# A three-block transformer kernel on one core: a second output tile begun later, earlier fills, roots by pairs, sums on GpSimd, and later weight copies before the last projection

## What is computed

```python
# first block
h = rms_norm(x, norm1_g); z = h @ w_in          # GLU input, q, k, v, gate logits
a = silu(rms_norm(conv31(val * sigmoid(gate)), conv_norm_g)); y_a = a @ w_conv_out
q, k = rms_norm per head; o = 3 dilated windows of attention, mixed by their sums
x = x + (g_a * y_a + g_b * (o @ w_attn_out)) @ w_out
x = x + (silu(u_gate) * u_val) @ w_down         # u = conv3(rms_norm(x) @ w_up)
# second block, layer 0 (sparse mixer): top-128 keys per query by 8 index heads
x = layer_norm(ALPHA * x + (o * silu(g)) @ w_out_a, ln_g0, ln_b0)
# layer 1 (stick-breaking mixer): weights from a cumulative log_sigmoid of the scores
x = layer_norm(ALPHA * x + (o * silu(g)) @ w_out_b, ln_g1, ln_b1)
```

## Time and profile before

| what | value |
|---|---|
| median of 3 runs | 1541.31 us (1541.19 to 1543.64) |
| the profiled execution | 1542.46 us |
| its span, first to last instruction | 1540.5 us |
| PE busy | 1515.3 us, 98% |
| DVE busy | 1152.0 us, 75% |
| ACT busy | 887.0 us, 58% |
| POOL busy | 768.8 us, 50% |
| granted TensorE clock | 0.998 |

### The profile page before, as it was taken

The page is one execution under the profiler, slowest core; times in us unless marked ns, Lnnn a source line. Parts: engine busy times, 40 slices in busy tenths (PEclk is TensorE's granted clock), DMA queues, the critical chain, the costliest instruction groups (busy, mean ns, idle before and its releaser), DMA issues.

```text
span 1540.5 us, 21821 instructions
## 1 busy us (share of the span) xinstructions
PE 1515.3 (98%) x7792; PEld 1293.6 (84%) x7792; DVE 1152.0 (75%) x2064; ACT 887.0 (58%) x1544; POOL 768.8 (50%) x726
## 2 busy tenths in 40 slices
PE   9999999999999999999999999999999999999997
PEld 7888899988888888888888888887888988888877
DVE  5999999998664687437717559967777828988977
ACT  6445788787433344324324464689995327777753
POOL 2232345435465477557747563456655424444443
PEclk9999999999999999999999999999999999999999
DMA  7889765665332222323222278856457945456551
GB/s 222 194 186 203 165 137 130 146 161 126 123 107 91 91 96 96 110 83 110 96 96 89 96 180 188 177 130 140 110 126 177 202 106 132 109 123 137 109 121 59
DMA packets 60299, 203.26 MB, mean 132 GB/s; under 512 B 6816, under 2 KB 9376, under 8 KB 60192
## 3 DMA queue, kind: packets, MB, share of 16 engines
q0 software_dynamic: 19008, 69.21, 26.3%
q1 hardware_dynamic: 40896, 132.14, 25.8%
q10 hardware_dynamic: 288, 0.52, 0.1%
HBM read 199.75 MB, written 2.10 MB: 131 GB/s over the span
## 4 chain that ended last, share of the span: by engine, by line
PE 84%; DVE 7%; ACT 5%; DMA 2%; issue 1%; POOL 1%; DVEq 0%; SPq 0%; POOLq 0%; ACTq 0%
PE bank L368 82%; PE bank L374 2%; DVE r L407 1%; DMA w_raw<-in_weights 1%; ACT k_both L378 1%; ACT prob L378 1%; ACT w_hi L378 1%; DVE pt_lo L395 1%; DMA w_lo<-in_weights 1%; DVE prob L1288 0%; ACT pt_hi L378 0%; DVE r L395 0%; DVE q_both L407 0%; DVE score L1875 0%; ACT soft L378 0%
## 5 line engine op out<-in xcount | busy, mean ns | idle before, releaser
L414 POOL TENSOR_TENSOR w_lo<-w_raw,w_hi 128x512 fp32r<-128x512 f32 (+1 forms) x190 | 278.5, 1485 | 210.3 <-ACT w_hi L378 210.3
L378 ACT ACTIVATE w_hi<-w_raw 128x1024 fp32r<-128x1024 f32 (+2 forms) x206 | 213.9, 1041 | 278.7 <-PE bank L368 253.3
L368 PE MATMUL bank<-x_hi,w_hi 128*128 128x512 f32 x872 | 346.6, 398 | 1.3 <-DVE k_lo_first L407 0.6
L368 PE MATMUL bank<-x_hi,w_lo 128*128 128x512 f32 x872 | 340.6, 391 | 0.6 <-DMA w_lo<-in_weights 0.4
L368 PE MATMUL bank<-x_lo,w_hi 128*128 128x512 f32 x872 | 340.1, 390 | 0.0
L368 PEld LDWEIGHTS bank<-x_hi,w_lo 128*128 128x128 f32 x872 | 163.7, 188 | 37.0 <-POOL w_lo L414 0.8
L368 PEld LDWEIGHTS bank<-x_hi,w_hi 128*128 128x128 f32 x872 | 163.9, 188 | 33.4 <-ACT k_both L378 1.0
L368 PEld LDWEIGHTS bank<-x_lo,w_hi 128*128 128x128 f32 x872 | 164.2, 188 | 29.8
L621 POOL DMA_DIRECT2D w_lo<-in_weights x132 | 117.0, 894 | 120.4 <-ACT w_lo L378 96.3
L368 PE MATMUL bank<-a_hi,w_hi 128*128 128x512 f32 x416 | 162.0, 389 | 0.0
L368 PE MATMUL bank<-a_hi,w_lo 128*128 128x512 f32 x416 | 161.8, 389 | 0.0
(11 more groups left out here) (230 smaller groups left out, 3403.5 us busy)
## 6 DMA issues: line engine op xcount, KB each, us to landing
w_raw<-in_weights SPq DMA_DIRECT2D x223, 512.0 KB, 3.4
w_lo<-in_weights POOLq DMA_DIRECT2D x132, 512.0 KB, 6.6
alibi<-in_alibi SPq DMA_DIRECT2D x16, 256.0 KB, 3.9
w_raw<-in_weights SPq DMA_DIRECT2D x8, 384.0 KB, 3.0
r<-in_x SPq DMA_DIRECT2D x8, 256.0 KB, 6.1
r<-in_x SPq DMA_DIRECT2D x4, 512.0 KB, 6.2
out_y<-r SPq DMA_DIRECT2D x16, 128.0 KB, 1.8
w_raw<-in_weights ACTq DMA_DIRECT2D x2, 256.0 KB, 4.2
```

Of the source, the lines that this page charges most:

```text
L368: return e.matmul(out, lhsT, rhs, start=start, stop=stop, skip_group_check=resumed)
L378: return self.act.run(lambda e: e.activation(out, in_, func, **kw), after, 0.07 + size(out) * 0.00086 + 0.09 * len(kw))
L414: return self.pool.run(lambda e: e.tensor_tensor(out, a, b, op), after, cost)
```

## The change

1. `two_tiles`: the first tile's units k run four ahead of the second's while the heads run, and the second tile takes its bank only at its first unit (`LEAD`).
2. `blank_scores`: the fills of `score` and `select` are put on DVE four planner microseconds after the feed-forward block, not at the start of `index_scores`.
3. `rsqrt`: y and g = m*y lie side by side, and one operation updates both; a root is 8 dependent operations (guess, g, then 2, 2 and 2) where it was 10.
4. `SHORT`: the planner counts at least 0.18 for a DVE operation of `v_tt`, `v_ts`, `v_stt` (before 0.07 for tiny ones). `LATER` is 0.5, not 1.5.
5. `sum_x`: in the last projection GpSimd adds x_hi and x_lo of tiles 4 to 7 (in the place of x_hi), so that `mix_evict` needs one DVE operation there, not two.
6. The ones used for column sums hold 1/D, so three multiplications by 1/D go; in `half_norm` a copy and a subtraction from the bank stand for two scalings and a subtraction.
7. `slot_ready`: `out_b` chunks in slots 5 and 6 also wait for the last pair's o parts.
8. `half_norm` of the last half: `keep_busy(3)` in front of the last tile's column sums. The first half's results start every 1.2, not 1.5.

```diff
-LATER = 1.5
+LATER = 0.5
+SHORT = 0.18
+LEAD = 4
@@ Block.__init__
+        self.x_sums = at("x_sums", 44, [KT, S])
@@ v_tt (v_ts and v_stt alike)
-        cost = 0.07 + size(out) * 0.00106
+        cost = max(SHORT, 0.07 + size(out) * 0.00106)
@@ slot_ready
         if self.slots[c] >= 3:
-            scores, weights = yield from self.know(self.phase_done, more_slots(self.plan[c])[0])
+            scores, weights, outputs = yield from self.know(self.phase_done, more_slots(self.plan[c])[0])
             after += yield from self.know(scores if self.slots[c] in AFTER_SCORES else weights, HEADS - 1)
+            if self.plan[c][0] == "out_b" and self.slots[c] in AFTER_WEIGHTS:
+                after += yield from self.know(outputs, PAIRS - 1)
@@ two_tiles
-        for key in keys:
-            begin(key)
-        for k in range(n_k - 1):
+        ahead = LEAD if self.in_heads else 0
+        order = sorted(((k, n) for k in range(n_k - 1) for n in range(len(keys))), key=lambda u: (u[0] if u[1] else u[0] - ahead, u[1]))
+        for k, n in order:
             while known is not None and k not in known and self.in_heads:
                 yield "idle"
-            for c, b in zip(cs, bs):
-                tok = self.unit(c, b, k, hi, lo, ready, False, used is not None and c == cs[-1])
...
+            while n == len(cs):
+                begin(keys[n])
+            second = used is not None and n == len(keys) - 1
+            tok = self.unit(cs[n], bs[n], k, hi, lo, ready, False, second)
...
@@ rsqrt(self, m, gy, t, ready)
+        g, y = gy[:, 0, :], gy[:, 1, :]
         tok = self.v_ts(y.bitcast(I32), m.bitcast(I32), -0.5, MAGIC, ALU.mult, ALU.add, [ready])
-        for _ in range(3):
-            tok = self.v_tt(t, y, y, ALU.mult, [tok])
-            tok = self.v_stt(t, t, -0.5, m, ALU.mult, ALU.mult, [tok])
-            tok = self.v_stt(y, t, 1.5, y, ALU.add, ALU.mult, [tok])
+        tok = self.v_tt(g, m, y, ALU.mult, [tok])
+        both = t.rearrange("p (o n) -> p o n", o=1).to_broadcast([P, 2, t.shape[-1]])
+        for n in range(3):
+            tok = self.v_stt(t, g, -0.5, y, ALU.mult, ALU.mult, [tok])
+            if n < 2:
+                tok = self.v_stt(gy, both, 1.5, gy, ALU.add, ALU.mult, [tok])
+            else:
+                tok = self.v_stt(y, t, 1.5, y, ALU.add, ALU.mult, [tok])
@@ rms
-        tok = self.v_ts(m, b.ap[:, 0:NT], 1.0 / D, eps, ALU.mult, ALU.add, [tok])
+        tok = self.v_ts(m, b.ap[:, 0:NT], eps, None, ALU.add, after=[tok])
@@ constants
-        self.ones_ready = self.v_fill(self.ones, 1.0)
+        self.ones_ready = self.v_fill(self.ones, 1.0 / D)
@@ index_scores, and a stream blank_scores started in sparse_mixer before the kiwi and qi tiles
+    def blank_scores(self):
+        yield self.hid_used
+        yield 4.0
         t0 = self.v_fill(self.score[:, :], 0.0, self.hid_used)
...
+    def index_scores(self):
+        t0 = self.got(self.blank, 0)
@@ sum_x, started by project_and_norm when last_norm is set, for tiles 4 to 7
+    def sum_x(self, used):
+        for c in self.x_summed:
+            hi, lo = self.x_hi[:, c, :].bitcast(F32), self.x_lo[:, c, :].bitcast(F32)
+            yield [used]
+            self.x_sum[c] = [self.p_tt(self.x_sums[:, c, :], hi, lo, ALU.add, [used])]
+            yield 1.4
@@ mix_evict
+        summed = (yield from self.know(self.x_sum, c)) if c in self.x_summed else []
+        x = self.x_sums[:, c, cols] if summed else self.x_hi[:, c, cols].bitcast(F32)
+        t = self.v_stt(u, x, 2.0 * ALPHA, b.ap[:, 0:n], ALU.mult, ALU.add, [t] + self.v_split[PAIRS - 1] + summed)
         b.release([t])
-        t = self.v_stt(u, self.x_lo[:, c, cols].bitcast(F32), 2.0 * ALPHA, u, ALU.mult, ALU.add, [t])
+        if not summed:
+            t = self.v_stt(u, self.x_lo[:, c, cols].bitcast(F32), 2.0 * ALPHA, u, ALU.mult, ALU.add, [t])
@@ half_norm
+        if half and self.last_norm:
+            yield from self.keep_busy(3)
         yield [t_u]
...
-        t1 = self.v_ts(mu, b.ap[:, 2 * half:2 * half + 2], 1.0 / D, None, ALU.mult, after=[t])
-        t2 = self.v_ts(m, b.ap[:, NT + 2 * half:NT + 2 * half + 2], 1.0 / D, None, ALU.mult, after=[t])
-        b.release([t2])
-        t = self.v_tt(w, mu, mu, ALU.mult, [t1])
-        t = self.v_tt(m, m, w, ALU.subtract, [t2, t])
+        t1 = self.v_copy(mu, b.ap[:, 2 * half:2 * half + 2], [t])
+        w_done = self.v_tt(w, mu, mu, ALU.mult, [t1])
+        t = self.v_tt(m, b.ap[:, NT + 2 * half:NT + 2 * half + 2], w, ALU.subtract, [t, w_done])
+        b.release([t])
@@ build
-        self.project_and_norm("out_b", 4, "ln_g1", "ln_b1", self.result, (1.5, 0.4))
+        self.project_and_norm("out_b", 4, "ln_g1", "ln_b1", self.result, (1.2, 0.4))
```

More of the change, by code:

```diff
@@ L397, in v_ts @@
     def v_ts(self, out, a, s1, s2, op0, op1=None, after=()):
-        cost = 0.07 + size(out) * 0.0008
+        cost = max(SHORT, 0.07 + size(out) * 0.0008)
         if op1 is None:
@@ L403, in v_stt @@
     def v_stt(self, out, a, s, b, op0, op1, after=()):
-        cost = 0.07 + size(out) * 0.00115
+        cost = max(SHORT, 0.07 + size(out) * 0.00115)
         if not (banked(a) or banked(b)):
@@ L676, in begin @@
             bs[-1].open = True
-        for key in keys:
-            begin(key)
-        for k in range(n_k - 1):
+        ahead = LEAD if self.in_heads else 0
+        order = sorted(((k, n) for k in range(n_k - 1) for n in range(len(keys))), key=lambda u: (u[0] if u[1] else u[0] - ahead, u[1]))
+        for k, n in order:
             while known is not None and k not in known and self.in_heads:
                 yield "idle"
-            for c, b in zip(cs, bs):
-                tok = self.unit(c, b, k, hi, lo, ready, False, used is not None and c == cs[-1])
-                if used is not None and c == cs[-1]:
-                    used[k] = [tok]
-                self.tick()
-                yield
+            while n == len(cs):
+                begin(keys[n])
+            second = used is not None and n == len(keys) - 1
+            tok = self.unit(cs[n], bs[n], k, hi, lo, ready, False, second)
+            if second:
+                used[k] = [tok]
+            self.tick()
+            yield
         for n, key in enumerate(late):
@@ L858, in spread, with rms @@
         return tok
-    def rms(self, acc, ready, eps, y):
+    def rms(self, acc, ready, eps, gy):
         yield ready
@@ L1053, in norm @@
             tok = yield from self.know(sums, KT - 1)
-            b, t, t_inv = yield from self.rms(acc[:, :], [tok, self.ones_ready, self.ident_in], 1e-6, self.h_inv)
+            b, t, t_inv = yield from self.rms(acc[:, :], [tok, self.ones_ready, self.ident_in], 1e-6, self.h_gy)
             self.wide_inv = self.ext[1]
@@ L1611, in conv_norm @@
                 yield from self.pad_known(c)
-            bank, bt, _ = yield from self.rms(self.ext[2][:, :], [self.conv_sq], 1e-6, self.stat_y)
+            bank, bt, _ = yield from self.rms(self.ext[2][:, :], [self.conv_sq], 1e-6, self.stat_gy)
             yield [bt]
@@ L1683, in norm @@
             tok = yield from self.know(self.sq_tok, KT - 1)
-            b, t, _ = yield from self.rms(self.ext[2][:, :], [tok], 1e-6, self.stat_y)
+            b, t, _ = yield from self.rms(self.ext[2][:, :], [tok], 1e-6, self.stat_gy)
             yield [t]
@@ L1824, in index_scores @@
             t0 = self.v_fill(self.score[0:64, a + 64:a + P], -BIG, [t0])
-        tok = {i: t0 for i in range(1, NT)}
         t1 = self.v_fill(self.select[:, 0:P], 0.0)
         self.select_ready[0] = [self.v_fill(self.select[0:64, 64:P], BIG, [t1])]
+        self.blank[0] = t0
+    def index_scores(self):
+        t0 = self.got(self.blank, 0)
+        tok = {i: t0 for i in range(1, NT)}
         rel_free = {}
@@ L1916, in ready @@
             return self.got(x_ready, k)
+        self.blank = {}
+        self.start(self.blank_scores())
         keys = [("kiwi", 0)] + [("qi", c) for c in range(4)]
@@ L1999, in project_and_norm @@
             self.start(self.half_norm(half, self.u_ready, self.u_sum, self.u_sq, *norm))
+        if self.last_norm:
+            self.x_summed = range(FIRST_HALVED[name], KT)
+            self.start(self.sum_x(self.chunk_done[self.plan.index(("gb", PAIRS - 1))]))
         hi, lo = (lambda k: self.o_hi[:, k, :]), (lambda k: self.o_lo[:, k, :])
```

26 lines of the change are left out of this document (15 added, 11 removed).

## The result

The changed kernel takes 1548.66 us (median of 6 runs, 1546.96 to 1552.74), the kernel before beside it 1542.26 (6 runs, 1541.19 to 1543.64): a ratio of 1.0038, 95% interval 1.0028 to 1.0048. It is slower by 6 us where 3.4 us were to be won.

What follows compares the result with a forecast made beforehand. PE, busy 98% of the span, was taken as the bound, with at most 25 us idle to win. Terms -2.2 + 0.4 - 0.1 - 1.2 + 0.2 - 0.5 = -3.4 gave a median of 1537.9 us, range 1534.7 to 1541.8.

Steps and rivals of the forecast that it cites:

- the rescheduling: LEAD in the two other mixers and SHORT everywhere move waits without a direction: 0, bounds -1.5 and +1.5 us.
- the cover of GpSimd's sums: Last projection: four additions of 1.29 us, 5.2 us on POOL, hidden under tiles 4 and 5 (5.7 us and more).
- the tail: Behind the last tile, from 1527: GpSimd's sums, constants, keep_busy(3) and pace give -0.1 us, bounds -0.9 and +0.9.
- Roots, LATER, SHORT: First heads move forward and fill waits: -1.2 us, bounds 0 and -2.0; separately +0.2 in the three RMS norms.
- the fills: Score fills move from the start of the index scores to idle DVE time: -0.5 us, bounds 0 and -1.6.
- The wait before k_both,q_both: First heads, near 178: this wait of PE was to be under 0.5 us if the prediction was right.
- The seam: Last mixer's heads to last projection: ACT wait goes, two units move ahead, o_lo shortens; -2.2 us, between -1.7 and -2.7.
- The bound of -0.2: Between the last mixer's heads and last projection: the gain may be only -0.2 us if filler is spread otherwise.
- Late copies: Last projection, tiles 6 and 7: later weight copies delay the adding DMAs; +0.4 us, bounds 0 and +2.8.
- The rival with the weight copies and the sums: Last projection: sums queued before copies on POOL, PE waits 8.0 us for two DMAs; slower, 1545.5 us; chance 0.12.

Runs made afterwards that it cites:

- e8: The changed kernel with SHORT back at 0.0, the old cost of short DVE steps: 1547.80 us, ratio 1.0025 to the kernel before.
- e11: The changed kernel with SHORT 0.0, old two_tiles, early weight copies, no GpSimd sums, no keep_busy(3), pace 1.5: 1544.84 us, ratio 1.0003.
- e12: The changed kernel with SHORT 0.0, early weight copies, no GpSimd sums, no keep_busy(3), pace 1.5; new two_tiles kept: 1545.03 us, ratio 1.0006.
- e14: The kernel before with the paired roots and the constant products alone: 1544.69 us, ratio 1.0012.
- e5: The kernel before with the new two_tiles (LEAD = 4) and the constant products alone: 1543.81 us, ratio 0.9996.
- e18: The kernel before with the constant products and the new end (later weight copies, GpSimd's sums, keep_busy(3), pace 1.2): 1546.81 us, ratio 1.0019.
- e6: The kernel before with the constant products alone (ones hold 1/D): 1542.91 us, ratio 0.9995.
- e15: The kernel before with the earlier fills of the scores and the constant products alone: 1542.93 us, ratio 0.9998.
- e1: The changed kernel without the later weight copies of the last projection's tiles 6 and 7: 1551.43 us, ratio 1.0053 to the kernel before.
- e3: The changed kernel with the old end: early weight copies, no GpSimd sums, no keep_busy(3), pace 1.5: 1550.71 us, ratio 1.0045.
- e17: The kernel before with the constant products and SHORT = 0.18, the bound on short steps: 1551.47 us, ratio 1.0049.
- e13: The changed kernel with early copies, no sums, no keep_busy(3), pace 1.5, old two_tiles, and SHORT only up to the first mixer's end: 1553.23 us, ratio 1.0061.
- e2: The changed kernel without GpSimd's four sums, DVE doing both steps again: 1552.19 us, ratio 1.0050 to the kernel before.
- e7: The changed kernel with the old two_tiles, so without LEAD: 1552.16 us, ratio 1.0047 to the kernel before.
- e9: The changed kernel with keep_busy(4) ahead of the first half's column sums in the last layer norm: 1549.14 us, ratio 1.0031.
- e16: The changed kernel with the 0.18 bound on short steps only up to the end of the first mixer: 1549.77 us, ratio 1.0040.
- e10: The changed kernel with the first half's small column sums of the last layer norm placed 18 projection matmuls later: 1549.65 us, ratio 1.0032.

## Why the prediction was wrong

The prediction failed on two steps: the rescheduling, priced at 0, and the cover of GpSimd's sums with the clock behind it, priced inside the tail's -0.1. Several terms were right in kind.

**Everything else that is rescheduled: 0, bounds -1.5 and +1.5.** This is the first step that failed. I let LEAD and the bound move waits about without a direction. The bound alone costs 7.6 us (1551.47 less 1543.9), where the whole term was to be at most +1.5. I had read it as a correction of the planner (a step costs 0.21 and is counted as less), which must help; I did not ask what all other places had been set to with the old costs. In its profile 4.4 us are the seam at 1213, whose mechanism is shown, and 2.4 the first mixer and the projection behind.

**Roots, LATER, SHORT: -1.2, and the fills: -0.5.** In the first mixer the gain was larger, -4.5 by 343, and the bound is what makes it hold there: without it (e8, e11, e12) the transposes wait 1.5 us for their data. That this is the shorter LATER is argued: e14, with the new roots and the old LATER, has no such wait and is 1.7 us ahead at 343. But 2.0 come back at once at the projection behind, where GpSimd's subtractions stand before w_lo, and 1.6 and 1.5 later. The roots alone measured 1.0012 (the term, with LATER, was -1.2 us and at worst 0), the fills 0.9998 against 0.9995 of the constants: no 0.5 us in them. The wait before k_both,q_both was 0.58, near the 0.5 that I named.

**The seam: -2.2.** Each single event came (the wait gone, seven units, o_lo 0.69), and the k = 7 units start 5.9 us behind the last weighing's start instead of 7.6. But the weighing itself slid by 1.2 us against the rest: with five units spent early, pt_lo, o_lo and sp_lo are waited for at 1480 to 1488 (2.2 us). The bound of -0.2 "if the filler is spread otherwise" was the near one: -0.5 by the table. In e5, with the old copies, it is +0.8.

**Late copies: +0.4, bounds 0 and +2.8.** PE waited 0.9 us at 1512.5. (The reckoning had tile 6 wanted from 1504.5 at the earliest; 1495.7 and 8.4 make 1504.1, so the upper bound was 3.2.) Not all four copies went first, as feared, but the second DMA did stand behind an addition that waited for VectorE. A size missed, inside its bounds.

**The tail: -0.1.** This is the second step that failed. The four sums were "hidden under tiles 4 and 5" in the prediction. That cover was gone: POOL was late by the copies, so tile 4's eviction was late, and the column sums waited 0.8 us, which was priced at nothing; the clock behind it cost 1.4 more in this profile and 2.5 in e18 (27 matmuls in 5.7 us where 0.119 each makes 3.2). The rival with the weight copies and the sums named this queue and the sign, but with a PE wait for the DMA of 8.0 us (0.9 was seen) and a forecast of 1545.5; the larger loss, the bound's, stood in no rival. What the tail had priced behind 1527 came to +0.4 by the table, inside its bounds.

**The range.** Its lower end was said to take the best bounds of seam, first heads and tail, -6.6; they make -5.6 (2.7, 2.0 and 0.9). The miss was on the other side, so nothing hangs on it.

**The parts do not add up.** By the ratios alone, and against the constants' 0.9995, LEAD costs 0.2 us, the fills 0.5, the roots 2.6, the bound 8.3, the new end 3.7: 15.3 together, where the change costs 6.6 on the same base (1.0038 less 0.9995). About half of the difference is seen in the profiles: at 343 the changed kernel is 4.5 us ahead, where bound, roots, fills and LEAD alone stand at +0.8, -1.7, +0.5 and -0.1, and LATER was in none of these. The other half is not traced, and the intervals of five ratios add up too. With the bound all ten kernels measured 1.0031 to 1.0061, without it the nine others 0.9995 to 1.0025.

No version beat the kernel before: e6 (0.9995), e5 (0.9996) and e15 (0.9998) equal it. What stays open: why the medians of e1 to e3 show nothing of the shorter end; LATER by itself, which was never tried; why the order drawn by the first mixer's bound has the waits near 914 and before 1122, and whether roots, LATER and bound with a hand-set queue for GpSimd near 380 would keep their 4.5 us.

## What to carry to other kernels

When a planner's cost of an operation is corrected, time the correction by itself before anything is built on it: delays and thresholds elsewhere may have been set against the old cost, as at the seam of e17 (42 matmuls put where 30 fitted), and here the correction alone cost as much as the whole change (1.0049 and 1.0038). Where PE is 98% busy, a wait of under 1 us beside one-column matmuls can cost over 3 us and not one (0.9 and 2.5 in e18), since the clock may fall behind it; look at the granted clock in windows of a few us, the mean over the span (0.998) shows nothing. Fill such a wait with matmuls that nobody needs, or place the small ones later: both kept the clock up here, for 1.0 to 1.5 us in the profiles. And for a transfer or a sum moved to a quiet engine, write down its queue at that time, not only its free time.

## What the runs showed of the hardware

The clock goes with most of the scatter between executions. Of the 29 of the kernel before that were timed beside e5 to e8, those with a mean granted clock of 0.998 took 1542.3 us on average (7), with 0.997 1543.9 (14) and with 0.996 1547.1 (7). The wait of 2.5 us for ACT r before the first o_hi unit stands in the same place of the order in the kernel before and in eight of the experiments: in five profiles the clock stayed up behind it, in four (e11, e13, e15, e18) it fell, and these lost 1.5 to 2.2 us more. e11's windows against e6's, with the same work:

```profile
1466.00:1472.00 6.00, 3.54 (x13) 2.60 (x12) 5.20 (x9) 4.17 (x10) 2.03 (x3) 0.86 0.28 87
1472.00:1476.00 4.00, 4.00 (x25) 3.81 (x23) 3.01 (x6) 3.44 (x8) 0.00 (x0) 0.79 0.02 6
```
```profile
1462.00:1468.00 6.00, 3.55 (x16) 2.60 (x15) 5.42 (x10) 4.29 (x10) 2.86 (x4) 1.00 0.23 87
1468.00:1472.00 4.00, 4.00 (x31) 3.92 (x30) 2.58 (x6) 3.74 (x8) 0.00 (x0) 1.00 0.02 6
```

The like holds at 392 (down in e2, e3, e7, e9 and e13, not in the changed kernel or e16) and at 1004 (down in e1, e2, e13 and e14). Beside the first half's small sums of the new end it fell in all eight profiles that had the waits, and in neither of the two (e9, e10) that had them filled or moved. So what a wait costs is its length, plus, with a chance, about as much again or more behind it; LEAD takes one of these chances away, but no median here shows that it pays.
